# Softmax attentions of a two-part transformer: two heads at a time, and dilated queries projected between the heads

## The reference

```python
p = masked_softmax(s, kpos[None, :] <= tpos[:, None])          # first and second block
...
q = (h @ w_q).reshape(bsz, seq, B_GROUPS, B_HEADS, B_HEAD_DIM)  # dilated: 3 groups, 16 heads, 64
q = _rms(q, q_gain[:, None, :]) * (B_HEAD_DIM ** -0.5)
...
s = jnp.einsum('birhd,bjrhd->bhrij', qb, kb).astype(f32) + biases[g][None, :, None]
s = jnp.where(valid[None, None], s, -jnp.inf)
lse = jax.nn.logsumexp(s, axis=-1)
...
wts = jax.nn.softmax(jnp.stack(lses), axis=0)                   # over the three groups
```

## Time and profile before

| | us |
|---|---|
| median of 3 runs | 2247.82 |
| lowest and highest | 2239.92, 2248.82 |
| profiled execution | 2246.6 |
| its span, first to last instruction | 2244.8 |
| TensorE busy, of the span | 2103.2 |
| VectorE, ScalarE, POOL busy | 1175.9, 982.7, 540.3 |

### The profile page before, as it was taken

One profiled execution on the slowest core, in us unless ns is written; L12 is line 12 of the kernel. 1 busy time (PEld: TensorE's weight loads), 2 busy tenths in 40 slices (PEclk: granted clock), 3 DMA queues, 4 the chain that ended last, 5 costly groups with the idle time before them and its releaser, 6 DMA issues.

```text
span 2244.8 us, 36902 instructions
## 1 busy us (share of the span) xinstructions
PE 2103.2 (94%) x15863; PEld 1981.9 (88%) x15863; DVE 1175.9 (52%) x1409; ACT 982.7 (44%) x1149; POOL 540.3 (24%) x152
## 2 busy tenths in 40 slices
PE   7888999989999998999886999999999989999999
PEld 6875799988789998999885999988999988669998
DVE  5325476665567666434786544424444332766433
ACT  4223344444443434444533444466444347544443
POOL 1100012322012231222142122452022356211222
PEclk9856799999999999999998999999999999899999
DMA  7300145434235443554421355535455534423553
GB/s 263 137 5 0 45 144 187 168 138 153 91 121 196 170 169 136 183 187 160 169 76 57 122 197 173 183 119 178 165 185 178 178 133 170 124 64 121 198 172 109
DMA packets 47329, 321.13 MB, mean 143 GB/s; under 512 B 5693, under 2 KB 6836, under 8 KB 9844
## 3 DMA queue, kind: packets, MB, share of 16 engines
q1 hardware_dynamic: 42644, 304.49, 38.6%
q0 software_dynamic: 2816, 9.44, 1.7%
q10 hardware_dynamic: 1760, 5.63, 0.7%
HBM read 318.41 MB, written 1.12 MB: 142 GB/s over the span
## 4 chain that ended last, share of the span: by engine, by line
PE 82%; DVE 11%; ACT 5%; issue 1%; DMA 0%; POOL 0%; ACTq 0%; SPq 0%; DVEq 0%
PE bank L368 23%; PE bank L370 22%; PE bank L369 22%; DVE lo L341 3%; PE bank L409 2%; PE bank L428 2%; ACT hi L335 1%; PE bank L431 1%; PE bank L411 1%; PE bank L444 1%; PE bank L1654 1%; PE bank L1435 1%; DVE arena L794 1%; ACT arena L1596 1%; DVE xl L765 1%
## 5 line engine op out<-in xcount | busy, mean ns | idle before, releaser
L368 PE MATMUL bank<-xh,hi 128*128 128x256 f32 x3208 | 930.5, 290 | 33.8 <-DVE xl L765 16.9
L369 PE MATMUL bank<-xl,hi 128*128 128x256 f32 x3208 | 916.9, 286 | 0.0
L370 PE MATMUL bank<-xh,lo 128*128 128x256 f32 x3208 | 916.7, 286 | 0.0
L341 POOL TENSOR_TENSOR lo<-ring,hi 128x2048 fp32r<-128x2048 f32 x100 | 468.6, 4689 | 1491.1 <-ACT hi L335 1491.1
L335 ACT ACTIVATE hi<-ring 128x2048 fp32r<-128x2048 f32 x291 | 550.9, 1899 | 473.3 <-PE bank L370 468.6
L341 DVE TENSOR_TENSOR lo<-ring,hi 128x2048 fp32r<-128x2048 f32 (+1 forms) x191 | 503.0, 2635 | 403.7 <-ACT hi L335 403.4
L368 PEld LDWEIGHTS bank<-xh,hi 128*128 128x128 f32 x3208 | 624.5, 195 | 47.8 <-issue 32.4
L369 PEld LDWEIGHTS bank<-xl,hi 128*128 128x128 f32 x3208 | 624.3, 195 | 4.9 <-issue 4.8
L370 PEld LDWEIGHTS bank<-xh,lo 128*128 128x128 f32 x3208 | 623.9, 194 | 0.2
L368 PE MATMUL bank<-gh,hi 128*128 128x256 f32 x1056 | 304.2, 288 | 20.2 <-DVE gl L701 20.2
L370 PE MATMUL bank<-gh,lo 128*128 128x256 f32 x1056 | 303.1, 287 | 0.0
(11 more groups left out here) (258 smaller groups left out, 2048.3 us busy)
## 6 DMA issues: line engine op xcount, KB each, us to landing
ring<-in_ffn_in SPq DMA_DIRECT2D x132, 1024.0 KB, 4.9
ring<-in_ffn_out SPq DMA_DIRECT2D x66, 1024.0 KB, 4.9
ring<-in_kv SPq DMA_DIRECT2D x24, 1024.0 KB, 4.9
ring<-in_hg_in SPq DMA_DIRECT2D x16, 1024.0 KB, 4.9
ring<-in_od_in SPq DMA_DIRECT2D x12, 1024.0 KB, 5.0
ring<-in_dq SPq DMA_DIRECT2D x12, 1024.0 KB, 4.8
ring<-in_ev_in SPq DMA_DIRECT2D x11, 1024.0 KB, 4.9
arena<-rel_rows POOLq DMA_DIRECT2D x16, 384.0 KB, 3.8
```

The costliest lines, as they stand in the source:

```text
L341: ns.tensor_tensor(lo[n % RING][:, 0:w], ring[n % RING][:, 0:w], hi[n % RING][:, 0:w].bitcast(F32), ALU.subtract).then_inc(lo_ok[lo_by[n]], 1)
L368: nc.tensor.matmul(out_, lh, rh, start=start, stop=False, **kw)
L369: nc.tensor.matmul(out_, lh, rl, start=False, stop=False, **kw)
L370: return nc.tensor.matmul(out_, ll, rh, start=False, stop=stop, **kw)
```

## The change

- A unit is now a pair of heads. The scores of both are issued alternately, the even head from the upper 64 partitions and the odd from the lower, into two of banks 0 to 2; the value products alternate too, into the two halves of one bank. Both heads have their own masks, maxima, exponentials, turns (banks 4 and 5) and copies. In the first two blocks the turns lag by two pairs, in the dilated stage by one, and there VectorE's division of a pair follows its maxima in the same turn (`late` is false).
- In the second block two pairs are held back, and the nine projections stand at two places of a unit: ahead of the scores (`early`) and behind them (`mid`).
- In the dilated stage the chunks are ordered by four heads (group 0, 1, 2 of heads 0 to 3, and so on). Three are projected ahead, nine between the pairs (`early` and `mid`), with square, mean, logarithm, exponential and norm chunk by chunk, so that each chunk has two table loads on ScalarE. DVE splits chunks 0 and 2, POOL the other ten. The relative biases are loaded from ScalarE's queue, four DMAs a pair. Three pairs are held back in the keys' buffer.

```diff
-            "dilated": [cols("dq", CW * c) for c in range(12)] + [cols("do", CW * c) for c in range(4)],
+            "dilated": [cols("dq", CW * (4 * g + hg)) for hg in range(4) for g in range(3)]
+            + [cols("do", CW * c) for c in range(4)],
...
+            elif b == "dilated":
+                lo_by += ["V" if c in (0, 2) or c >= 12 else "P" for c in range(len(streams[b]))]
...
+            def scores(i):
...
+                for g in range(ns):
+                    w = i * ns + g
+                    if w >= 1:
+                        pe.wait_ge(*s.at("masked", 2 * w - 1))
+                    for q0, k1, c0, c1 in ((P, T, 0, T), (0, P, T, 384)):
+                        for e in range(2):
+                            sub = un["subs"][e][g]
+                            last = nc.tensor.matmul(soft_bank(w, e)[:, c0:c1], sub["q"][:, q0:q0 + P], sub["k"][:, 0:k1],
+                                                    start=True, stop=one)
+                        if not one:
+                            for e in range(2):
+                                last = nc.tensor.matmul(soft_bank(w, e)[:, c0:c1], cum[e][0], cum[e][1][:, 0:k1],
+                                                        start=False, stop=True)
+                    last.then_inc(soft_sem["qk"], 1)
...
+            def turned(j):
+                for g in range(ns):
+                    w = j * ns + g
+                    for e in range(2):
+                        act.wait_ge(*s.at("turned", 2 * w + e + 1))
+                        if w >= 2:
+                            act.wait_ge(*s.at("pv", w - 1))
+                        nc.scalar.activation(s.pt[w % 2][e], bank[4 + e][:, 0:384], ACT.Copy).then_inc(soft_sem["pt"], 1)
 
             for i in range(U + s.lag):
...
+                s.hook(s.before, "act", i, act)
+                u, j = (i - 1 if s.late else i), i - s.lag
+                exps_first = s.late or i in s.mid["pe"]
+                if exps_first and 0 <= u < U:
+                    exps(u)
+                s.hook(s.mid, "act", i, act)
+                if j >= 0:
+                    turned(j)
+                if not exps_first and 0 <= u < U:
+                    exps(u)
                 if j >= 1:
                     pair_out(j - 1)
...
+                s.hook(s.after, "act", i, act)
...
+            early = {0: 4, 1: 6, 2: 7, 3: 9, 4: 10, 5: 12}
+            mid = {0: 5, 2: 8, 4: 11}
...
+            early = {0: 3, 1: 5, 2: 6, 3: 8, 4: 9, 5: 11}
+            mid = {0: 4, 2: 7, 4: 10}
...
+            def pe_mid(i):
+                def run(pe):
+                    if i in early:
+                        mean(pe, early[i])
+                    if i in mid:
+                        project(pe, mid[i])
+                return run
...
+            def act_early(i):
+                def run(act):
+                    squares(act, early[i])
+                    roots(act, early[i])
+                    if i < 7:
+                        biases_in(act, i + 1)
+                return run
...
+            soft.mid["act"] = {i: lambda act, c=c: squares(act, c) for i, c in mid.items()}
+            soft.after["act"] = {i: lambda act, c=c: roots(act, c) for i, c in mid.items()}
```

More of the change, by code:

```diff
@@ L390, in __init__ @@
-                self.pv = sem(tag + "_pv")
-                self.oh = sem(tag + "_oh")
-                self.o = sem(tag + "_o")
+                self.mid = {"pe": {}, "dve": {}, "act": {}}
+                self.after = {"pe": {}, "dve": {}, "act": {}}
+                self.turn_after = {}
+                n, pairs = len(units), 1 + max(un["pair"] for un in units)
+                gates = sum(un.get("gate") is not None for un in units)
+                adds = {"qk": n * ns, "masked": 2 * n * ns, "max": 2 * n, "exp": 2 * n,
+                        "rec": n * (1 if late else 2) + gates, "p": 2 * n, "turned": 2 * n * ns, "pt": 2 * n * ns,
+                        "pv": n * ns, "oh": pairs - len(held), "o": pairs}
@@ new lines, in __init__, with at, hook, soft_bank @@
+                self.base = {k: soft_total[k] for k in adds}
+                for k, m in adds.items():
+                    soft_total[k] += m
+            def at(self, k, n):
+                return soft_sem[k], self.base[k] + n
+            def hook(self, where, eng_name, i, eng):
+                if i in where[eng_name]:
+                    where[eng_name][i](eng)
+        def soft_bank(w, e):
+            return bank[(2 * w + e) % 3]
+        def soft_out(pair):
+            return bank[6 + pair % 2][:, 0:T]
@@ L512, in soft_dve @@
+            lows = 0
+            for i in range(U + (1 if s.late else 0)):
+                s.hook(s.before, "dve", i, dve)
+                if i - s.lag - 2 >= 0:
+                    pair_low(lows)
+                    lows += 1
+                if i < U:
+                    masks(i)
+                s.hook(s.mid, "dve", i, dve)
+                if s.late and i >= 1:
                     weights(i - 1)
-            for u in range(U - 1 - s.lag, U):
+                elif not s.late:
+                    weights(i)
+                s.hook(s.after, "dve", i, dve)
@@ L514, in soft_dve @@
+            for u in range(lows, U):
                 pair_low(u)
@@ L571, in pe_chunk @@
                 for e in range(0, width, P):
+                    if half is not None and e:
+                        half()
                     m = min(P, width - e)
@@ L1830, in pe_part @@
-            def pe_part(pe):
-                pe_n(pe)
-                pe.wait_ge(s["lin"], 11)
+            for p in range(8):
+                units.append({"pair": p, "first": True, "last": True,
+                              "ready": (done, 3 * (p // 2) + 3), "wait": (rel_in, 64 * (p + 1)),
+                              "subs": [[{"q": DQ[pb:pb + DH, p // 2 % 2, 2 * g + p % 2, :], "k": DK[pb:pb + DH, 8 * g + p, :],
+                                         "v": [DV[:, t, g * D + (2 * p + e) * DH:g * D + (2 * p + e + 1) * DH]
+                                               for t in range(2)],
+                                         "add": REL[e][:, g, :]} for g in range(3)] for e, pb in enumerate((0, DH))]})
@@ new lines, in make_dilated @@
+            soft.after["pe"] = {i: lambda pe, c=c: mean(pe, c) for i, c in mid.items()}
+            soft.before["dve"] = {i: lambda dve, c=c: take_out(dve, c) for i, c in early.items()} | {6: held_low}
+            soft.mid["dve"] = {i: dve_mid(i) for i in early}
+            soft.after["dve"] = {i: lambda dve, c=c: norm(dve, c) for i, c in mid.items()}
+            soft.before["act"] = {i: act_early(i) for i in early} | {6: held_high}
+            soft.mid["act"] = {i: lambda act, c=c: squares(act, c) for i, c in mid.items()}
```

520 lines of the change are left out of this document (279 added, 241 removed).

## The result

The changed kernel takes **2210.87 us** (median of 4, 2210.24 to 2212.35), the kernel before 2243.95 us (median of 4 beside it, 2239.92 to 2248.82): ratio **0.9857**, 95% interval 0.9838 to 0.9877, 33 us less. Forecast were 2227 and a range of 2198 to 2248. So the direction and the range held; the gain is half as large again as the 21 us forecast. One execution of the changed kernel differs from another by up to 2 us, one of the kernel before by up to 9.

What follows compares the result with a forecast made beforehand. TensorE, busy 92 to 99% in the three stages, was taken to bound the kernel. First block -21, second -15, dilated stage +15 gave -21: 2227 us on the median's basis, range 2198 to 2248.

Steps and rivals of the forecast that it cites:

- First block, -21: First block at 1.2 GHz: pairing heads' scores and values takes the stage from 65.4 to 44 us.
- the bound of -28: First block's larger-gain bound: clock rises to 2.4 GHz and VectorE's 32.3 us set the time.
- Second block, -15: Second block at 2.4 GHz: pairs at 3.24 us save 18 us, net 15 after idle time in the tail.
- Dilated stage, +15: Dilated stage: serial units sum to 194.9 us against 189.8, plus 10 for the clock; bounds -10 and +45.
- the clock term: Dilated stage: waits in the new loop lower TensorE's clock, costing 10 us; bounds 0 and 40.
- The loop's mechanism: Dilated units: TensorE's next projection waits behind turns and values, these for copies, these behind exponentials; 21.2 or 24.3 us a unit.
- the four issues in series: Dilated loop: four bias DMA issues on ScalarE, 0.44 us each, stand ahead of the pair's exponentials.
- The first: Rival: dilated loop overlaps better, TensorE's work sets 155 us instead of 205, total 2176; chance 0.14.
- the second: Rival: the clock costs twice what was taken, or DMA issues are dear, total 2236 to 2248; chance 0.16.
- The third: Rival: dilated loop stays at 1.2 GHz through units 0 to 5, +45 for that stage, total 2257; chance 0.10.
- The fourth: Rival: opposite halves run one after the other, first two blocks keep about 4 us each, total 2254; chance 0.04.
- The rule on taking results out of PSUM: Skill rule: tiling speeds TensorE alone, PSUM removal may bound; weighed as changing nothing by rate, by order only the dilated stage.

Runs made afterwards that it cites:

- the run with the copies first: Changed kernel with ScalarE, in dilated units 0 to 5, copying a pair's turned matrices ahead of the next pair's exponentials: 2205.98 us, ratio 0.9844.
- the third loop: Changed kernel, dilated loop reordered, GpSimd issuing biases and splitting chunks 12 and 13, projections taken out and last mean done earlier, tail reordered: 2192.14 us.
- the reordered loops: Changed kernel with the dilated loop reordered, then biases on GpSimd, then traced waits taken away, then four steps moved: 2220.72, 2209.98, 2192.14, 2187.41 us.
- the last loop: The third loop with GpSimd splitting chunks 12 and 13 before pair 6's biases, also chunk 14, and held pairs split after pair 7's masks: 2187.41 us.

## Why the forecast was right, and where it was not

**First block, -21, measured -31.9.** The count of operations fits: at half clock, with the overlap, the stage would be 53.1 less 9, 44 us, as forecast (an estimate from the run with the scores apart). The step that failed is the clock, which I took at 0.50 "nearly to its end" because the old stage had it there. I had the case as the bound of -28 and in the list of what would make the gain larger, and gave it too little: a stream whose own shape had changed can't be priced at the clock of the old one. The measured gain passes even that bound, which was mis-sized twice: 65.4 less 32.3 is 33 and not 28, unless 5 us are added that the text doesn't name, and VectorE's work isn't the 32.3 us of before but 27.18, in 99 instructions for 115. With the clock at 1.00 VectorE does become nearly the bound: 27.18 us busy of 33.5, 9.86 of 10 in the middle. The two scores experiments show the adjacency at work in both directions: added to the kernel before it brings the clock, taken from the changed kernel it loses it.

**Second block, -15, measured -15.2.** 86.9 us for 87. A pair's scores were reckoned at 1.67 us and take 1.77, its two heads' turns at 0.77 and take 0.77 (tail of the block, TensorE):

```profile
541.92 0.70 PE L428 MATMUL bank<-arena 64*128 64x256 f32 x4
...
543.69 0.29 PE L475 MATMUL bank<-ident,arena 128*128 128x128 f32 x1
...
544.46 0.65 PE L449 MATMUL bank<-arena 128*64 128x256 f32 x4
```

**Dilated stage, +15, measured +21.8 (18 by the run with the old dilated stage).** The sum was 48.0 + 112.2 + 34.7 and 10 for the clock. Measured are 44.2 to unit 1 (1816.1), 124.4 to the scores of pair 6 and 43.0 for the tail: 3.8 less, 12.2 more and 8.3 more, 16.7 in all where the clock term had 10. The loop's mechanism was right, as the waits and the run with the copies first show. Its longest wait was 4.7 us and not 6.8, since I had set the four issues in series; what followed the wait was dearer, since TensorE's turns and values ran at half clock behind it. The tail was reckoned without the clock. VectorE's weights of pair 6 end 21.1 us into it, where I had 18.7, those of pair 7 another 15.1 later, where I had 11.9, and the turns and values behind them take 6.8 us for 4.1. The end of the weights of the two pairs in VectorE's timeline, and TensorE's waits for masks (1940.5 to 1983.5):

```profile
1961.16 0.47 DVE L525 TENSOR_SCALAR arena<-arena 128x384 f32<-128x384 f32 x1
1976.29 0.47 DVE L525 TENSOR_SCALAR arena<-arena 128x384 f32<-128x384 f32 x1
```

```profile
PE bank L428 <- DVE arena L498: 10.5, 4, 5.0
```

The term that was too small is the clock's. A mean of 0.90 over the 124.4 us of the loop and of 0.80 over the tail means that a fifth and two fifths of the time were at half clock; if TensorE was busy in all of it, that cost 12 and 9 us, an upper estimate, against the 10 that I took. The issues that I had in series made up for part of it.

GpSimd's splits beside VectorE I had priced at nothing, because they run while VectorE waits. That held by its result, but not by its reason. In the changed kernel a step of VectorE's weights stands beside a split and takes 5.07 us in place of 0.75 (VectorE's and GpSimd's timelines below), and one of unit 0 takes 4.72; TensorE waited for neither (the turns of those weights come a pair later). In the third loop such a step did cost, 5.6 us.

```profile
1859.98 5.07 DVE L524 TENSOR_SCALAR arena<-arena 128x768 f32<-128x768 f32 x1
1859.97 4.53 POOL L344 TENSOR_TENSOR lo<-ring,hi 128x2048 fp32r<-128x2048 f32 x1 [13.03 <-ACT hi L338]
```

**Rivals.** The first (an overlapping loop, TensorE setting the time, 155 us for the stage, 35 less than before) did not come in the changed order, nor in any of the reordered loops; the last gets the stage from 212.5 to 186.4. It was over-hopeful even there: with no wait over 1.6 us up to pair 6 a unit with two projections takes 23.4 us (1835.2 to 1858.6), 21.2 of them work of TensorE, where 79 + 56 made it 20.2, and the start and the tail are 30.3 and 43.8 us, where the rival had 20 over and above TensorE's work. Of the second, the clock did cost more than I took, but the issues cost less, and the time didn't rise to its 2236. The third (1.2 GHz through the loop) did not happen: 0.91 on average. The fourth is refuted by the eight score records in one head's time. The rule on taking results out of PSUM bore out by order only, as weighed: ScalarE's copies had the rate and stood in the wrong place.

**The sum.** -31.9 - 15.2 + 21.8 is -25.3, against 36.2 between the two spans and 33 between the medians; the rest lies in code that doesn't change, 6.6 us of it ahead of the first stage in this pair of profiles. Two terms of opposite sign were each too small (by 11 and by 7), so that the 2227 is nearer than its parts by luck. And 4 of the 16 us by which it is too high are its base: it started from 2247.8, the median of three runs of the kernel before, where four make 2243.95.

## What to carry to other kernels

Put the products that can run in opposite halves of the array right next to each other, and price the stage at both clocks: here score products put next to each other, with the units reordered for it and nothing else changed, brought 28 us of stage time, about half by running together and half by the clock (an estimate). When work is moved between the stages of a loop over three engines, write down for each engine's queue what stands ahead of the operation that the next unit waits for; a wait taken away uncovers the next one, and only a trace after each step (2221, 2210, 2192, 2187 us) showed which. Split a change into its parts before tuning it: one of the two halves of this one cost 18 us, and it took four reordered loops to win that back; the last of them isn't told apart from simply leaving that half out.

## What the runs showed of the hardware

- TensorE's granted clock stayed at 0.50 (1.2 GHz) where the profile counts the engine as busy for 20.00 of 20.00 us (kernel before, 200 to 220). It was 1.00 where it counts 8.02 of 10 (changed kernel, 200 to 210) and also where it counts 10.00 of 10.00 (kernel before with adjacent scores, 210 to 220). What the engine did in the first: score products of one head at a time, in the other two those of two heads running together. The Trainium skill, "TensorE: Matmul & The Clock Gate", section "What's actually happening", calls 1.2 GHz the state of an idle engine, which activity lifts; the busy time in these rows, as the profile counts it, doesn't agree with it, and the measurement decides.
- Operations of VectorE from SBUF to SBUF stood still for as long as GpSimd's split ran: one with two tensor inputs (L1918) took 9.31 us for 0.75 beside two splits in a row, ones with a single tensor input (L524, L525) 5.07 for 0.75 and 4.72 for 0.47 beside one. VectorE's masks, which read PSUM, kept their time beside a split (1.02 for two, 1903.83 in the last loop, with GpSimd at a split from 1902.96 to 1907.50). The Trainium skill, "SBUF — State Buffer", section "SBUF: two separate sides", says that the two engines hold a pair of ports by turns and for a whole instruction, an operation of VectorE with two SBUF inputs among them; for L1918 the trace agrees, and VectorE got the pair only behind both splits.
- A pair's four bias transfers, issued by GpSimd, take 3.04 us to issue. For pair 6 of the last loop they take 6.3 and 7.0 us to land (medians of the larger and the smaller ones); in the changed kernel with the transfers back on GpSimd the medians over the stage are 4.7 and 4.8. A mask that needs them has to come that much later.
